# Five TensorE products instead of six per weight block, joined by VectorE before the read

## What is computed

```
h = h + rmsnorm(mixer(rmsnorm(h)))
h = h + rmsnorm(conv_ffn(rmsnorm(h)))          # up: 1024 -> 2 x 2816, down: 2816 -> 1024
h = h + sigmoid(rmsnorm(h) @ Wg) * (p[i] @ Wp) # per-layer embedding (ple, pw)

mlstm_mixer: proj = xn @ w_in; q, k, v, o, gates = proj; ... ; y = (sigmoid(o) * h) @ w_out
swa:         q, k, v = rope(xn @ w_in); ... ; y = o @ w_out
conv_ffn:    u = xn @ w_up; c = conv_b + sum_j up[:, j:j+T] * conv_w[j]; (silu(c[:F]) * c[F:]) @ w_down
```

## Time and profile before

| what | us |
|---|---|
| median of 3 runs | 1296.81 (1296.8 to 1296.97) |
| span of the profiled execution, first to last instruction | 1294.8 |
| TensorE busy | 1287.4 (99%) |
| VectorE busy | 891.1 (69%) |
| ScalarE busy | 594.0 (46%) |
| GpSimd busy | 75.0 (6%) |
| TensorE's share of the chain that ended last | 95% |

### The profile page before, as it was taken

One profiled execution on the slowest core, in us unless ns is written; L12 is line 12 of the kernel. 1 busy time (PEld: TensorE's weight loads), 2 busy tenths in 40 slices (PEclk: granted clock), 3 DMA queues, 4 the chain that ended last, 5 costly groups with the idle time before them and its releaser, 6 DMA issues.

```text
span 1294.8 us, 25277 instructions
## 1 busy us (share of the span) xinstructions
PE 1287.4 (99%) x10786; PEld 1254.7 (97%) x10786; DVE 891.1 (69%) x1602; ACT 594.0 (46%) x1060; POOL 75.0 (6%) x117
## 2 busy tenths in 40 slices
PE   9999999999999999999999999999999999999998
PEld 8999989999999999999999978999999999999998
DVE  7899776987777774223897787688777777422385
ACT  6214565544444443223855677554444444222381
POOL 1112230000100000000031020000000000000000
PEclk9999999999999999999999999999999999999999
DMA  5435521213343233222314232311322323322231
GB/s 199 155 100 194 198 99 53 103 58 106 95 105 94 87 111 114 90 90 78 138 59 148 68 97 81 113 52 50 98 94 87 98 84 110 114 90 90 79 130 67
DMA packets 35616, 131.84 MB, mean 102 GB/s; under 512 B 4516, under 2 KB 5260, under 8 KB 35184
## 3 DMA queue, kind: packets, MB, share of 16 engines
q1 hardware_dynamic: 29664, 111.33, 26.8%
q0 software_dynamic: 5408, 18.26, 4.3%
q10 hardware_dynamic: 432, 0.64, 0.2%
HBM read 121.26 MB, written 10.08 MB: 101 GB/s over the span
## 4 chain that ended last, share of the span: by engine, by line
PE 95%; DVE 3%; ACT 1%; DMA 0%; issue 0%; ACTq 0%; DVEq 0%
PE tile L1177 24%; PE tile L1181 24%; PE tile L1179 24%; PE tile L1187 5%; PE tile L1188 5%; PE tile L1189 4%; PE tile L1649 1%; PE side L1187 1%; PE side L1188 1%; PE side L1189 1%; PE sums L1226 0%; DMA raw<-in_w_kv 0%; PE sums L1700 0%; PE sums L1348 0%; PE sums L1707 0%
## 5 line engine op out<-in xcount | busy, mean ns | idle before, releaser
L756 ACT ACTIVATE wH<-raw 128x1024 fp32r<-128x1024 f32 (+1 forms) x190 | 210.9, 1113 | 377.4 <-DMA raw<-in_w_up 145.9
L1177 PE MATMUL tile<-xH,wH 128*128 128x260 f32 x1798 | 362.7, 283 | 0.1
L1181 PE MATMUL tile<-xH,wL 128*128 128x260 f32 x1798 | 362.4, 283 | 0.0
L1179 PE MATMUL tile<-xL,wH 128*128 128x260 f32 x1798 | 361.8, 283 | 0.0
L1832 DVE TENSOR_TENSOR wL<-raw,wH 128x1024 fp32r<-128x1024 f32 (+1 forms) x190 | 245.7, 1294 | 154.5 <-ACT wH L756 150.4
L1177 PEld LDWEIGHTS tile<-xH,wH 128*128 128x128 f32 x1798 | 277.1, 188 | 3.5 <-issue 3.0
L1181 PEld LDWEIGHTS tile<-xH,wL 128*128 128x128 f32 x1798 | 277.2, 188 | 0.0
L1179 PEld LDWEIGHTS tile<-xL,wH 128*128 128x128 f32 x1798 | 276.4, 188 | 0.0
L1880 DVE SCALAR_TENSOR_TENSOR u<-tile,rstd 128x520 f32<-128x520 f32 x96 | 67.2, 700 | 119.5 <-PE tile L1181 119.4
L1177 PE MATMUL tile<-hidH,wH 128*128 128x260 f32 x616 | 124.3, 283 | 0.0
L1181 PE MATMUL tile<-hidH,wL 128*128 128x260 f32 x616 | 123.8, 282 | 0.0
(11 more groups left out here) (446 smaller groups left out, 1913.9 us busy)
## 6 DMA issues: line engine op xcount, KB each, us to landing
raw<-in_w_up SPq DMA_DIRECT2D x88, 512.0 KB, 3.6
raw<-in_w_down SPq DMA_DIRECT2D x32, 704.0 KB, 4.1
raw<-in_w_ple SPq DMA_DIRECT2D x16, 512.0 KB, 5.6
raw<-in_w_qo SPq DMA_DIRECT2D x12, 512.0 KB, 3.6
raw<-in_w_qkv SPq DMA_DIRECT2D x12, 512.0 KB, 3.5
raw<-in_w_kv SPq DMA_DIRECT2D x10, 512.0 KB, 3.7
cring<-in_c_in POOLq DMA_DIRECT2D x8, 512.0 KB, 4.8
out_c_s<-cring POOLq DMA_DIRECT2D x8, 512.0 KB, 3.2
```

Source lines behind the costliest of these rows:

```text
L756: nc.scalar.activation(wH[j][:, 0:n], raw[j][:, 0:n], ACT.Copy).then_inc(s_high, 1)
L1177: nc.tensor.matmul(out[:, q, 0:HT], wh, x[0][:, k, tokens(q)], start=first, stop=False)
L1179: nc.tensor.matmul(out[:, q, 0:HT], wh, x[1][:, k, tokens(q)], start=False, stop=False)
L1181: mm = nc.tensor.matmul(out[:, q, 0:HT], wl, x[0][:, k, tokens(q)], start=False, stop=last)
```

## The change

1. `wide_product` takes the place of `product` in most chunks. The high and low parts of an input now lie in one tensor (xHL, pxHL, hidHL, pHL), so that one matmul can take the first 256 columns of both: 512 columns, high results in the left half of the bank, low ones in the right half. The other 264 columns take three matmuls into the second bank, and wL times the first 256 columns of xH is added to the right half of the first bank. The results of the first 256 columns are then the sum of the bank's two halves.
2. `set_apart` (ScalarE) copies the left half to SBUF when the chunk is done, and `join` (VectorE) adds it into the right half. After that columns 256 to 775 of the double bank are the 520 results in a row, and the read takes them from there. The copy's place in SBUF is one for all chunks of a stage, so a copy also waits for the join before it.
3. Which chunks are wide is given by `wide`: 136 chunks (counting the two chunks of a result of down as one), with 1284 weight blocks.
4. The copy's place in the early stages is that of the constant `band`, which GpSimd now loads after down0 instead of SyncE at the start.
5. In qkv ScalarE's `rotate` moves behind the other work of its chunk, which stays as it was.

```diff
+def wide(stage, c):
+    if stage[:2] == "up":
+        return c >= SPLIT
+    if stage[:4] == "down":
+        return c < KT - 1
+    if stage[:3] == "ple":
+        return SPLIT <= c < KT - 1
+    return stage == "kv" and c >= 2 or stage in ("qo", "qkv") and c < COUNT[stage] - 1
...
+        xHL = sb("xHL", [P, 2, KT, T], F32R)
+        xH, xL = xHL[:, 0], xHL[:, 1]
...
+            def set_apart(stage, c):
+
+                if wide(stage, c):
+                    j = JOIN[stage, c]
+                    act.wait_ge(s_mm, CHUNK0[stage] + (2 * c + 2 if stage[:4] == "down" else c + 1))
+                    if j:
+                        act.wait_ge(s_joined, j)
+                    nc.scalar.activation(apart(stage), bank(stage, c)[:, 0, 0:WIDE], ACT.Copy).then_inc(s_apart, 1)
...
@@ ScalarE, stage qo
                 if c == 11:
                     sigmoids(4, 7)
+                set_apart("qo", c)
@@ ScalarE, stages up
                     elif c:
                         hid_high(c // 2 - 1)
+                    set_apart(up, c)
                     act.wait_ge(s_read, READ0[up] + c + 1)
@@ ScalarE, stages down
-                        act.wait_ge(s_mm, CHUNK0[down] + c + 1)
-                        src = bank(down, k)[:, :, 0:HT]
+                        set_apart(down, k)
+                        act.wait_ge(s_joined, JOIN[down, k] + 1)
+                        src = results(down, k)
...
+            def wide_product(c, w, x, k, out, first, last):
+
+                wh, wl = (t[SLOT[c]][:, w * P:w * P + P] for t in (wH, wL))
+                right = out[:, 1, 0:T - WIDE]
+                nc.tensor.matmul(out[:, 0, :], wh, x[:, :, k, 0:WIDE], start=first, stop=last, skip_group_check=True)
+                nc.tensor.matmul(right, wh, x[:, 0, k, WIDE:T], start=first, stop=False)
+                nc.tensor.matmul(right, wh, x[:, 1, k, WIDE:T], start=False, stop=False)
+                nc.tensor.matmul(out[:, 0, WIDE:2 * WIDE], wl, x[:, 0, k, 0:WIDE], start=False, stop=last, skip_group_check=True)
+                return nc.tensor.matmul(right, wl, x[:, 0, k, WIDE:T], start=False, stop=last)
...
+            def join(stage, c):
+
+                if wide(stage, c):
+                    j, low_results = JOIN[stage, c], bank(stage, c)[:, 0, WIDE:2 * WIDE]
+                    dve.wait_ge(s_apart, j + 1)
+                    nc.vector.tensor_tensor(low_results, low_results, apart(stage), ALU.add).then_inc(s_joined, 1)
+
+            def scaled_read(stage, c, dst, scale=1.0):
+
+                join(stage, c)
                 dve.wait_ge(s_mm, CHUNK0[stage] + c + 1)
...
```

More of the change, by code:

```diff
@@ L79 @@
         _c += 1
+def wide(stage, c):
[6 more added lines that the diff above has]
+    return stage == "kv" and c >= 2 or stage in ("qo", "qkv") and c < COUNT[stage] - 1
+JOIN = {}
+for _s in ORDER:
+    for _k in range(KT if _s[:4] == "down" else COUNT[_s]):
+        if wide(_s, _k):
+            JOIN[_s, _k] = len(JOIN)
 READ0, YREAD0, ACC0, SUM, MA0 = {}, {}, {}, {}, {}
@@ L404, in depth, with apart, results, as_results @@
             return next(DEPTHK[s] for s in reversed(ORDER) if CHUNK0[s] <= c)
+        def apart(stage):
+            if stage == "qkv":
+                return acc[:, 0:WIDE]
+            return apart_late[:] if stage[:3] == "ple" else apart_early
+        def results(stage, c):
+            if wide(stage, c):
+                return bank(stage, c)[:].rearrange("p q t -> p (q t)")[:, WIDE:WIDE + T]
+            return bank(stage, c)[:, :, 0:HT]
+        def as_results(stage, c, ap):
+            return ap if wide(stage, c) else halves(ap)
         def halves(ap):
@@ L1186, in half_product @@
                 wh, wl = (t[SLOT[c]][:, w * P:w * P + P] for t in (wH, wL))
-                nc.tensor.matmul(out, wh, x[0][:, k, tokens(q)], start=first, stop=False)
-                nc.tensor.matmul(out, wh, x[1][:, k, tokens(q)], start=False, stop=False)
-                return nc.tensor.matmul(out, wl, x[0][:, k, tokens(q)], start=False, stop=last)
+                nc.tensor.matmul(out, wh, x[:, 0, k, tokens(q)], start=first, stop=False)
+                nc.tensor.matmul(out, wh, x[:, 1, k, tokens(q)], start=False, stop=False)
+                return nc.tensor.matmul(out, wl, x[:, 0, k, tokens(q)], start=False, stop=last)
             def weights_ready(c):
@@ L1201, in chunk @@
                         pe.wait_ge(s_xr, XSET[stage] + k + 1)
-                    mm = product(c, k, x, k, out, k == 0, k == KT - 1)
+                    mm = (wide_product if wide(stage, k0) else product)(c, k, x, k, out, k == 0, k == KT - 1)
                     if k < KT - 1:
@@ L1542, in feed_forward @@
                     chunk(up, c, X)
-                d0, hid = CHUNK0[down], (hidH, hidL)
+                d0, hid = CHUNK0[down], hidHL
                 for k0 in range(KT - 1):
@@ L1556, in feed_forward @@
                         for k in range(DKH):
-                            mm = product(c, k, hid, part * DKH + k, bank(down, k0), k == 0 and part == 0,
-                                         k == DKH - 1 and part == 1)
+                            mm = wide_product(c, k, hid, part * DKH + k, bank(down, k0), k == 0 and part == 0,
+                                              k == DKH - 1 and part == 1)
                         mm.then_inc(s_mm, 1)
@@ L1789, in _ @@
                     pe.wait_ge(s_soft, g)
-                chunk("qkv", c, (pxH, pxL), between=attend)
+                chunk("qkv", c, pxHL, between=attend)
                 if c == 2:
@@ L2299, in feed_forward @@
                         k = c // 2
+                        join(down, k)
                         dve.wait_ge(s_yr, YREAD0[down] + k + 1)
```

66 lines of the change are left out of this document (39 added, 27 removed).

## The result

| what | before | after |
|---|---|---|
| median of the runs, us | 1296.80 (1296.53 to 1296.97) | 1327.22 (1326.53 to 1328.75) |
| ratio after / before, 95% interval | | 1.0237 (1.0223 to 1.0252) |
| span of the profiled execution, us | 1294.8 | 1325.9 |
| mean granted TensorE clock | 1.00 | 0.995 |

A forecast was written before the change was run, and what follows sets the result against it. TensorE's matmul stream, busy 99%, was taken as the bound. Terms 14.7+2.6+0.8-3.6-0.7+1.0+0.7 = +15.5 us on a span of 1294.8 gave 1310.3, with 2.0 for launch and end 1312; range 1302 to 1321.

The forecast's parts named there:

- Sign and main mechanism: Whole kernel 15.5 us slower; in qo and up the copy's place behind other ScalarE work makes the helper loop decide.
- Rival (e): In qo the copies do not stand in the way; TensorE gains nearly all of 15 us: 1282, chance 0.04.
- Six make 720 ns ... plus five gaps if the gap belongs to the product: Each wide block: five products save one 11.7 ns gap against six; 15.0 us of TensorE work over 1284 blocks.
- rival (a): The gap belongs to columns, so nothing is saved in down and ple: 1316, chance 0.09.
- (d): Extra 11.7 ns come from weight loads that longer products cover; five products take 667 ns: 1293, chance 0.09.
- (f): Two thirds of the way to (d), a block of 681 ns: 1299, no difference, chance 0.03.
- Stages up ... +1.3 per layer: In up: late sixth and seventh chunks cost 2.7 us, some 19 pairs at 11.47 us give back 1.2, first chunks 0.2.
- rival (b): Helper loop in up is longer, 0.10 us more for copy and join: +8 in both layers, 1320, chance 0.12.
- 0.4 twice for the first low weights of down: Entering down, the first low weights cost 0.4 us in each of two layers.
- Stage qo, +14.7 forecast: Helper loop sets qo's pace, reads at least 7.47 us apart; stage ends at 170.5 instead of 155.79, kv's savings included.
- My own signs of being wrong: Wrong if TensorE idle in qo under 3 us, down block under 690 ns, read far from 0.9 us after chunk.
- +1.0 for the late input: ple's VectorE falls some 1.6 us behind in layer 0, so the next stage's last input comes late: +1.0 us.

The follow-up runs named there:

- experiment 1: The changed kernel with ScalarE's copy and VectorE's join left out everywhere, five products kept (results incomplete): 1293.45 us, ratio 0.9976 to the kernel before.
- experiment 3: The changed kernel with ScalarE's copy in stage qo moved ahead of outer product, decays and sigmoids: 1313.79 us, ratio 1.0135 to the kernel before.
- experiment 4: The changed kernel with six products, no copy and no join in both stages up: 1316.89 us, ratio 1.0157 to the kernel before.
- Experiment 7: The changed kernel with ScalarE's copy early in qo and also first in both stages up: 1302.71 us, ratio 1.0052 to the kernel before.
- experiment 5: Kernel wide in down alone (1295.3 us), its 512-column product cut into two in down0, four in down1: 1328.63 us, ratio 1.0247 to before.
- experiment 9: The changed kernel with extra 240-column products filling TensorE's waits before qo's memory queries: 1326.58 us, ratio 1.0232 to the kernel before.

## Why the forecast was right, and where it was wrong

- **Sign and main mechanism: right.** Stage qo costs the most because the copy stands behind the outer product (experiments 1 and 3), with distances between reads that were forecast to 0.1 us in five cases of seven. So do the copies in up (experiments 4 and 7). Rival (e) falls with this.
- **The step "Six make 720 ns ... plus five gaps if the gap belongs to the product": wrong.** I took a gap measured at one width, 11.7 ns, for a price per product. At 512 columns it is 19.3, and the block takes 716 to 719 ns, not 708: nearly rival (a), which I gave 0.09. It cost the forecast 2.3 us in down, 0.6 in ple, 0.9 in qkv and 1.2 at the entry of qo, where fourteen chunks of kv and qo were to be 1.3 us shorter together and were 0.1 shorter. Rival (a) itself was priced too low at 1316, since it counted down and ple alone: with qkv and the entry of qo it is some 1319. In experiment 1, without any helper, the change saves 3.2 us where I had put 15.0. The Trainium skill (TensorE: Matmul & The Clock Gate, Back-to-back issue gap), which I weighed and set aside, gives 2.5 ns beside the columns for a product by itself, by my estimate from it 3.2 us in all. Experiment 1 agrees with that sum, but in part by luck: a block saves 1.7 ns in kv and up and 5.0 in down, and no float32r product here has a gap of 2.5 ns.
- **Rivals (d) and (f): excluded.** Experiment 1, without any helper, saves 2.5 ns per block where (d) needed 53. Weight loads do set a floor, 111 ns at 128 and 192 columns, but it lies below the 120 of 260 columns, so taking loads away frees nothing at these widths. PEld busy 250 of 250 us was a full row and not a bound. The same page of the Trainium skill (section LDWEIGHTS) gives columns of the weights over 1.2 GHz, 107 ns for 128; the floor of 111 and the loads 0.11 us apart in experiment 5 fit it.
- **"Stages up ... +1.3 per layer": the terms at the start right, the steady pace wrong.** The sixth and seventh chunk came 1.59 and 1.18 late in up0, forecast 1.48 and 1.2. But a pair takes 11.55 us and not 11.47. From the join's start to the read's it is 0.54 (396.53 to 397.07) and not 0.45: the handover behind the join takes 0.11 instead of 0.03; the copy is 0.03 to 0.04 shorter. That turns 1.2 us given back into 0.3 taken, rival (b) at half its size. In up0 two chunks in the middle cost 0.9 more. There GpSimd issues a transfer (L759) from 370.13 to 373.57, and two operations of VectorE that otherwise take 0.16 and 0.43 us, the taps (L2333) and the join, take 2.05 and 1.32; the first ends at 373.54. The same happens in experiment 3. The kernel before has such a stretched operation too (L2262 from 351.10 to 352.90, the issue from 349.48 to 352.92), but there VectorE had idle time to lose. No run takes the transfer away, so this cause is read from the rows and not shown. Measured 3.9 and 3.0.
- **"0.4 twice for the first low weights of down": incomplete.** The 0.4 came, and 1.9 behind it each time. I had written that in up the helper loop sets the pace. Then VectorE's read falls behind the chunk's end until the low weights, which VectorE makes behind it, are only just in time. At the end of up0 the lag is 3.7 us, and the next stage, which needs the last result of the loop, pays for it. Experiment 7 takes the lag away, and the wait goes with it; experiment 4 likewise. That is 3.8 us for both layers, for which the sum had no term.
- **Stage qo, +14.7 forecast, 17.8 measured with kv.** The fourth read starts at 106.89 and not 105.3: 1.2 by the product's price, 0.2 because the whole stream starts 0.25 later, 0.2 by VectorE's lag (3.3 us behind the chunk, forecast 3.1). 1.2 more by the clock (experiment 9); the remaining 0.3 is not assigned. TensorE's waits in qo were 11.8 us in all, where some 15 were forecast.
- **My own signs of being wrong.** TensorE's idle time in qo is above 3 us and a block of down above 690 ns, as they should be. But the read was to follow a chunk by about 0.9 us, and it follows by 3.3 to 3.7 in most of up and by 1.0 to 5.4 in qo. For qo the forecast's own loop says as much; for up this sign was there, and it is the lag that the entry of down pays.
- **qkv:** +1.0 for the late input, as forecast; +1.7 instead of +0.7 inside the stage, 0.9 of it because the chunks do not get shorter. The rest was not taken apart.

By the table the misses are 3.1 (kv and qo) + 4.3 (up) + 3.8 (entering down) + 2.3 (down) + 0.6 (ple) + 1.0 (qkv) = 15.1 us, which is what lay between forecast and result in the traces, 30.55 against 15.5. Some 5 us of it are the product's price, 5 the lag at the entries of down and the clock, and most of the rest is up's slower pace and the two chunks in its middle.

## What to carry to other kernels

Price an instruction at the size it will have, not by a gap taken at another size: two widths make a line, one width makes none, and a line holds only down to the floor (here 111 ns). If a change makes a helper loop the slower one, count twice: the loop's pace while it runs, and the lag that stands at its end, which the first consumer in the next stage pays. And before giving up an exchange that adds work to an in-order engine, look at its place in the order: the same change costs 30 us with the copies in one order and 6 in another.

## What the runs showed of the hardware

- A float32r product with 128 weight columns added 111 ns to its block at 128 and at 192 columns alike; the weight loads of the 128-column products started 0.11 us apart (experiment 5). Between 260 and 512 columns it costs 0.45 ns per column, where columns/2.4 gives 0.417.
- The same five products take 719.2 ns per block in kv and up and 716.2 in down, also without any copy or join (experiment 1); six products take 720.8 and 721.2. What makes this difference stays open; it was not tried.
- TensorE's granted clock fell to 1.2 GHz around waits of 3.0, 3.2 and 2.6 us in a stream that was otherwise dense. Around a wait of 2.0 us at the same place of stage qo it fell in experiment 7's trace and not in experiment 3's or the changed kernel's, so the same wait can go either way. In a stage that waits anyway three falls cost 1.2 us together (experiment 9).
- While GpSimd issued one transfer for 3.44 us, an operation of VectorE stretched to the end of the issue: 2.05 us instead of 0.16 in the changed kernel, and 1.80 in the kernel before. It cost time only where VectorE had none to spare.
- A VectorE add that reads and writes PSUM, 256 columns, takes 0.43 us, and the read behind it starts 0.54 after the add's start; ScalarE's copy of 256 columns out of PSUM takes 0.36 to 0.39.
